# The statistics sums and the first two weight tiles of a projection, interleaved on TensorE

## The reference

```python
def rmsnorm(x, g):
    xf = x.astype(jnp.float32)
    y = xf * lax.rsqrt(jnp.mean(xf * xf, axis=-1, keepdims=True) + EPS)
    return (y * g.astype(jnp.float32)).astype(x.dtype)
...
x = x + 0.5 * rmsnorm(swiglu(rmsnorm(x, g[0]), w_ffn_gu[l, 0], w_ffn_down[l, 0]), g[1])
```

## Time and profile before

| | us |
|---|---|
| runs | 3531.46, 3548.50, 3548.51 |
| median | 3548.5 |
| span of the profiled execution | 3542.4 |
| TensorE busy in it | 3241.2 (91%) |
| VectorE, ScalarE busy | 1478.8 (42%), 1160.0 (33%) |
| mean granted TensorE clock | 0.950 of full |

### The profile page before, as it was taken

How to read it: one execution, slowest core, us unless ns; L and a number is a source line. 1 busy time by engine, 2 the same in 40 slices (tenths; PEclk the granted TensorE clock), 3 DMA queues, 4 the chain that set the end, 5 groups by cost and what they waited for, 6 DMA issues and landing times.

```text
span 3542.4 us, 55784 instructions
## 1 busy us (share of the span) xinstructions
PE 3241.2 (91%) x22328; PEld 2962.0 (84%) x22328; DVE 1478.8 (42%) x2113; ACT 1160.0 (33%) x1624; POOL 269.6 (8%) x364
## 2 busy tenths in 40 slices
PE   6999996998898898998999889999898878899997
PEld 5799996777677776798999879999896666899996
DVE  4444325655555512325443334443432051444423
ACT  3433323433333332324332214332222242333322
POOL 0000000211221110000000000000001101100000
PEclk9999997999989998999999999999999988999998
DMA  5422321222222223322232233332321611223321
GB/s 190 130 85 87 89 89 53 74 70 65 61 62 61 79 91 107 115 87 65 84 88 88 67 105 93 89 89 88 102 83 43 216 42 49 69 83 89 87 88 52
DMA packets 444917, 305.86 MB, mean 86 GB/s; under 512 B 12516, under 2 KB 415644, under 8 KB 444700
## 3 DMA queue, kind: packets, MB, share of 16 engines
q1 hardware_dynamic: 421780, 231.03, 22.3%
q0 software_dynamic: 19744, 69.48, 5.7%
q10 hardware_dynamic: 3328, 4.47, 0.4%
HBM read 282.73 MB, written 22.20 MB: 86 GB/s over the span
## 4 chain that ended last, share of the span: by engine, by line
PE 87%; DVE 7%; ACT 2%; issue 2%; DMA 1%; ACTq 0%; POOL 0%; SPq 0%; DVEq 0%; POOLq 0%
PE PS L894 64%; PE PS L945 5%; PE PS L932 2%; PE PS L1060 2%; PE PS L1072 1%; PE PS L1185 1%; PE PS L1033 1%; PE PS L1011 1%; DVE yT L1377 1%; DVE rb L1362 1%; PE PS L1187 1%; PE PS L1050 1%; PE PS L1250 1%; PE PS L1118 1%; PE PS L1197 1%
## 5 line engine op out<-in xcount | busy, mean ns | idle before, releaser
L894 PE MATMUL PS<-hH,whi 128*128 128x272 f32 x4048 | 842.8, 289 | 12.8 <-DVE hL L1373 7.6
L894 PE MATMUL PS<-hH,wlo 128*128 128x272 f32 x4048 | 837.8, 288 | 0.0
L894 PE MATMUL PS<-hL,whi 128*128 128x272 f32 x4048 | 837.0, 288 | 0.0
L1358 DVE TENSOR_TENSOR wlo<-raw,whi 128x1024 fp32r<-128x1024 f32 (+2 forms) x401 | 488.5, 1218 | 807.8 <-ACT whi L503 799.8
L503 ACT ACTIVATE whi<-raw 128x1024 fp32r<-128x1024 f32 (+2 forms) x401 | 413.1, 1030 | 766.3 <-PE PS L894 666.7
L894 PEld LDWEIGHTS PS<-hH,whi 128*128 128x128 f32 x4048 | 638.0, 189 | 14.9 <-issue 13.1
L894 PEld LDWEIGHTS PS<-hL,whi 128*128 128x128 f32 x4048 | 638.5, 189 | 0.0
L894 PEld LDWEIGHTS PS<-hH,wlo 128*128 128x128 f32 x4048 | 634.5, 189 | 0.0
L894 PE MATMUL PS<-H,whi 128*128 128x272 f32 x1984 | 411.9, 289 | 5.7 <-DVE L L1761 2.5
L894 PE MATMUL PS<-H,wlo 128*128 128x272 f32 x1984 | 411.0, 289 | 0.0
L894 PE MATMUL PS<-L,whi 128*128 128x272 f32 x1984 | 410.4, 288 | 0.0
(11 more groups left out here) (312 smaller groups left out, 3427.8 us busy)
## 6 DMA issues: line engine op xcount, KB each, us to landing
raw<-in_w_ffn_gu SPq DMA_DIRECT2D x176, 512.0 KB, 3.7
kvr<-in_cache_mem_kv POOLq DMA_DIRECT2D x32, 1024.0 KB, 5.5
raw<-in_w_in_a SPq DMA_DIRECT2D x57, 512.0 KB, 3.7
raw<-in_w_ffn_down SPq DMA_DIRECT2D x64, 448.0 KB, 3.3
rawm<-in_w_mem_kv SPq DMA_DIRECT2D x32, 512.0 KB, 4.2
raw<-in_w_ffn_down SPq DMA_DIRECT2D x32, 512.0 KB, 3.6
raw<-in_w_out_a SPq DMA_DIRECT2D x24, 512.0 KB, 3.5
raw<-in_w_in_b SPq DMA_DIRECT2D x20, 512.0 KB, 3.6
```

Source lines behind the costliest of these rows:

```text
L894: mm = pe.matmul(PS[:, bank + h, 0:HT], w[:, slot, k * P:(k + 1) * P], x(k0 + k)[:, h * HT:(h + 1) * HT], start=first and k == 0 and w is ...
L1358: dve.tensor_tensor(wlo[:, slot, 0:nk * P], src, whi[:, slot, 0:nk * P].bitcast(F32), ALU.subtract).then_inc(s["w_lo"], 1)
```

## The change

TensorE has a new function `first_pair`, which replaces the statistics and the first two units of each of the five projections: for each block it adds the square's sum and then that block's products for unit 0 and for unit 1. The last two blocks' sums come before their products. For this the split of unit 1 is moved ahead on both engines; the reciprocal is moved behind the split of unit 2; and the first pass of the gate/up loop is written out on ScalarE and VectorE. `residual` keeps the order of its additions, with one split ahead of it.

```diff
@@ ScalarE, end of narrow (the stage before)
+                if ahead is not None:
+                    split(ahead + 1, (ahead + 1) % 2)
@@ ScalarE, ffn
+                if f == 0:
+                    split(d.u0 + 1, (d.u0 + 1) % 2)
                 folded_h(gain(l, 4 * f))
...
+                        begun = first and b == 0
+                        if begun:
+                            split(u + 2, d.u0 % 2)
+                        else:
+                            split(u + 1, (d.u0 + 1) % 2)
                         act.wait_ge(evac[2 * b], i + e0[2 * b] + 2)
                         act.activation(sg[:, b, :], sg[:, b, :], ACT.Silu).then_inc(s["silu_done"], 1)
-                        split(u + 2, d.u0 % 2)
+                        if not begun:
+                            split(u + 2, d.u0 % 2)
...
-                step_loop(act, d.n, gu)
+                gu(0, True)
+                step_loop(act, d.n, gu, 1)
@@ TensorE
+            def first_pair(d):
...
+                for j in range(2):
+                    pe.wait_ge(evac[j], n.ev[j] + 1)
+                pe.wait_ge(s["w_lo"], d.u0 + 4)
+                def block(j, k):
+                    pe.wait_ge(*h_ready(k))
+                    mm = product((d.u0 + j) % 2, k, hH[:, k, :], hL[:, k, :], 2 * j, k == 0, k == KD - 1)
+                    if k == KD - 1:
+                        mm.then_inc(s["w_mm"], 1)
+                for k in range(KD):
+                    pe.wait_ge(s["sq_ready"], n.sq + k + 1)
+                    sums(sqf[:, k % 2, :], k == 0, k == KD - 1).then_inc(s["sq_used"], 1)
+                    if k < KD - 2:
+                        block(0, k)
+                        block(1, k)
+                for j in range(2):
+                    block(j, KD - 2)
+                    block(j, KD - 1)
...
@@ TensorE, dense
+                        if j < begun:
+                            seen[b] += 1
+                            continue
+                        if begun and j == 2:
+                            pe.wait_ge(s["rt_ready"], n.norm)
@@ VectorE, residual
+                if g_next:
+                    split(ahead + 1, (ahead + 1) % 2)
                 inverse()
@@ VectorE, ffn
+                d = ph["gu", l, f]
                 if f == 0:
+                    split(d.u0 + 1, (d.u0 + 1) % 2)
                     for k in range(KD):
                         folded_low(k, gain(l, 0))
                     n.t += KD
-                inverse(rtf)
...
+                        begun = first and b == 0
+                        if begun:
+                            split(u + 2, d.u0 % 2)
+                            inverse(rtf)
+                        else:
+                            split(u + 1, (d.u0 + 1) % 2)
                         dve.wait_ge(s["w_mm"], u + 3)
                         dve.tensor_tensor(halves(sg[:, b, :]), PS[:, 4 * b:4 * b + 2, 0:HT], halves(rb[:, :]), ALU.mult).then_inc(evac[2 * b], 1)
-                        split(u + 2, d.u0 % 2)
+                        if not begun:
+                            split(u + 2, d.u0 % 2)
@@ VectorE, in_b
+                    split(ph["in_b"].u0 + 2, ph["in_b"].u0 % 2)
                     inverse(rtf)
-                    queries(ph["in_b"], dst=M1, first=12, scale=HD ** -0.5)
+                    queries(ph["in_b"], 2, dst=M1, first=12, scale=HD ** -0.5)
```

More of the change, by code:

```diff
@@ L596, in to_h, with narrow @@
                 highs(y_of, hH_of, KD)
-            def narrow(d, early=0, last=False):
+            def narrow(d, early=0, last=False, ahead=None):
                 e = list(n.ev)
@@ L678, in ffn @@
                 dn = ph["down", l, f]
-                narrow(dn, last=(l, f) == (DEPTH - 1, 1))
+                narrow(dn, last=(l, f) == (DEPTH - 1, 1), ahead=ph["in_b"].u0 if (l, f) == (1, 0) else None)
             for l in range(DEPTH):
@@ L815, in _ @@
                     n.t += KI
-                    narrow(d, 2)
+                    narrow(d, 2, ahead=ph["gu", 0, 1].u0)
                 else:
                     folded_h(gain(1, 2))
-                    queries(ph["in_b"])
+                    queries(ph["in_b"], early=1)
                     queries(ph["qm", 1])
@@ L885, in _, with product @@
             n = Place()
+            def product(slot, k, hi_k, lo_k, bank, first, final):
+                for w, x in ((whi, hi_k), (whi, lo_k), (wlo, hi_k)):
+                    for h in range(2):
+                        mm = pe.matmul(PS[:, bank + h, 0:HT], w[:, slot, k * P:(k + 1) * P],
+                                       x[:, h * HT:(h + 1) * HT],
+                                       start=first and w is whi and x is hi_k, stop=final and w is wlo)
+                return mm
             def products(slot, nk, k0, hi, lo, bank, first, final, ready=None):
@@ L891, in products, with dense, body @@
                         pe.wait_ge(*ready(k0 + k))
[L892 to L897, removed]
-                return mm
-            def dense(d, hi, lo, pos=lambda j: j, ready=None, summed=False):
+                    mm = product(slot, k, hi(k0 + k), lo(k0 + k), bank, first and k == 0, final and k == nk - 1)
+                return mm
+            def first_pair(d):
+                n.t += KD
+                n.unscaled += KD
+                for j in range(2):
[15 more added lines that the diff above has]
+                    block(j, KD - 1)
+                n.sq += KD
+                n.norm += 1
+            def dense(d, hi, lo, pos=lambda j: j, ready=None, summed=False, folded=False):
+                if folded:
+                    first_pair(d)
                 e = list(n.ev)
-                def body(i):
+                def body(i, begun=0):
                     seen = [0] * 4
@@ L916, in body @@
                                      None if j else ready).then_inc(s["w_mm"], 1)
-                step_loop(pe, d.n, body)
+                if folded and d.tiles > 2:
+                    body(0, 2)
+                step_loop(pe, d.n, body, int(folded))
                 if summed:
+                    n.norm += 1
                     pe.wait_ge(evac[2], n.ev[2] + 1)
@@ L1080, in ffn @@
             def ffn(l, f):
-                folded_stats()
-                dense(ph["gu", l, f], hH_of, hL_of, ready=h_ready)
+                dense(ph["gu", l, f], hH_of, hL_of, folded=True)
                 dense(ph["down", l, f], lambda k: H24[:, k, :], lambda k: L24[:, k, :], ready=lambda k: (s["mid_lo"], n.mid + k + 3), summed=True)
@@ L1231, in _ @@
                 else:
-                    folded_stats()
-                    dense(ph["in_b"], hH_of, hL_of, ready=h_ready)
+                    dense(ph["in_b"], hH_of, hL_of, folded=True)
                     dense(ph["qm", 1], hH_of, hL_of)
```

38 lines of the change are left out of this document (17 added, 21 removed).

## The result

The kernel after takes 3565.4 us (median of 5 runs, 3563.6 to 3570.4), the kernel before 3548.5 (5 runs, 3531.5 to 3548.7). The ratio is 1.0063, 95% interval 1.0047 to 1.0079. The forecast was 3571.5, range 3553 to 3585, "slower by over 0.5%" at 0.63. The low end of the interval lies just under that half per cent, the middle above it. The ratio is taken over all the runs; the two medians are 16.9 us or 0.48% apart. Two of before's five runs lie 13 to 17 us under the others, and in 21 and 22 later runs its median was 3546.3 and 3545.9, 19 to 20 us under the changed kernel's. So the direction and the size are as forecast; that the ratio comes out at 0.63%, and not nearer to half a per cent, is owed in part to before's two low runs.

What follows compares the result with a forecast made beforehand. TensorE was taken as the bound, busy for 91% of the span. Work moved forward (-13.0), waits behind the pair (18.9 + 5.6) and clock falls (+11.5) gave +23.0 on 3548.5 us: 3571.5, range 3553 to 3585.

Steps and rivals of the forecast that it cites:

- slower by over 0.5%: Whole kernel: a time above 3566.2 us, chance 0.63.
- end of the pair: When units 0 and 1 are done at five projection starts: changes -0.2, -3.3, -0.1, -4.3 and -5.1 us, together -13.0.
- moved forward, with the clock of (0,0): Five projection starts: pairs end 13.0 us earlier together, against 1.2 us for the clock's fall at (0,0).
- unit 3 after the pair's end, four times: Four gate/up projections: unit 3 starts 10.8 us after the pair's end instead of 6.06, with TensorE idling 3.65.
- unit 2 of in_b after the pair's end: In in_b, unit 2 waits for unit 0's bank, read after the reciprocal, and starts 5.6 us after the pair.
- lost behind the pair: Waits after the pair's end: 18.9 us over four gate/up projections plus 5.6 us in in_b.
- clock, without (0,0): Clock falls after waits behind the pair: 8.0 us before unit 3 in four projections, 2.3 in in_b.
- The pass: At five starts, sums and first pair take 19.5 us at full clock, plus half of the half-clock time.
- The path behind unit 0: From unit 0's end: split of unit 2, reciprocal, gate tile, split of unit 3; unit 3 starts 12.3 us after.
- The clock: TensorE falls to half clock after the new idle times: 8.0 + 2.3 + 1.2 = +11.5 us, bounds 0 and 18.
- The clock holds: Rival: the idle times come, but the clock does not fall after them; +11.5 us, 3560; chance 0.22.
- The lock step: Rival: in the pass, squares wait for sums behind two blocks' products; 2.4 us a projection, +12, 3583; chance 0.10.

Runs made afterwards that it cites:

- e2: Changed kernel with a plain copy in place of the reciprocal of the five folded norms: 3541.7 us, ratio to before 0.9992.
- e5: Changed kernel with the split of unit 3 moved ahead of unit 0's gate tile on both engines: 3546.8 us, ratio to before 0.9998.
- e6: Changed kernel with only two blocks of unit 1 woven in, its other six after unit 0: 3543.9 us, ratio to before 0.9995.
- e3: Changed kernel with unused extra matmuls in TensorE's waits, 10 before unit 2 in in_b, 6 before unit 3 elsewhere: 3558.3 us, ratio to before 1.0042.
- e7: Changed kernel with e4, e5 and e6 together: 3531.8 us, ratio to before 0.9958.
- e8: e7 with unit 1's split after the second block at (0,0) and (1,0), TensorE waiting for it only before unit 1: 3531.9 us, ratio to before 0.9956.
- e9: e8 with sums first and tiles after, not woven, in gate/up of (0,0) and (1,0): 3531.3 us, ratio to before 0.9962.
- e4: Changed kernel with the reciprocal ahead of the split of unit 2 in VectorE's queue, gate/up and in_b: 3558.4 us, ratio to before 1.0045.

## Why the prediction was right, step by step

Times of the kernel after are moved back by the distance of the stage's first restart from that of before (0.55, 9.03, 12.02, 18.12 and 19.21 us), so that they stand beside the prediction's.

| term | predicted | measured |
|---|---|---|
| end of the pair, (0,0) | 163.4, and 1.2 of clock | 165.2 |
| (0,1) | 1624.2 | 1624.0 |
| (1,0) | 2160.6 | 2160.7 |
| in_b | 2577.6 | 2578.0 |
| (1,1) | 3106.0 | 3105.9 |
| moved forward, with the clock of (0,0) | -11.8 | -11.1 |
| unit 3 after the pair's end, four times | 10.8 | 10.5 |
| unit 2 of in_b after the pair's end | 5.6 | 5.3 |
| lost behind the pair | +24.5 | +23.0 |
| clock, without (0,0) | +10.3 | +9.3 |
| sum | +23.0 | +21.2 |

The forward ends are 1624.2 - 1627.5 and so on; the measured ones, against the same readings of before, are +1.6, -3.5, 0.0, -4.0 and -5.2. The sum of the terms, 21.2, meets the five stages' 21.5.

- **The pass.** The sum of sums and blocks at 0.92 and 0.757, with half of the half-clock time on top, gave four ends within 0.4 us. Its miss is (0,0): the start came at 144.06 in place of 143.9, and the clock fell there for 3.4 us (1.7) where I had taken 1.2 between nothing and more. The half-clock times in it, 5.8, 4.9 and 3.7, are the 6.1 and 4.0 of the earlier trace rows less the delay of each start, which the prediction doesn't say; that the spell ends where it ended before was an assumption. The kernel after shows 5.8, 5.1 and 4.9, and 4.9 at (1,1), where only one spell is left, as forecast. So at in_b 1.2 us more were at half clock than assumed, and that is the whole miss there.
- **The path behind unit 0.** Its order and members were as predicted. It is 0.3 us shorter; I had added handovers of 0.1 and 0.2 at each step. The wait before unit 3 came out at 3.14 us instead of 3.65. e2, e5 and e6 cut it, break it up and start it earlier, and each takes back 16 to 24 us.
- **The clock.** I took 2.0 for each wait before unit 3, because 3.65 was longer than the five in the trace; at 3.14 it wasn't longer than the 3.36 there, and it cost 1.7 each time, as after 2.6 us at the earlier trace rows. "The clock holds" (0.22) didn't happen: e3 shows what it would have brought, 8.1. The Trainium skill (TensorE: Matmul & The Clock Gate, "HAM oscillation — how this bites in real kernels") has each wait between bursts pay anew. The trace agrees at the five waits of 3.1 us and more behind the pairs; after the four of 1.1 us, and after the 3.36 us at 2085.64, nothing was paid.
- **The lock step** (0.10) didn't come: the pass at (0,1) took 22.35 us where 22.4 were forecast, with no wait of over 0.35 us in it.
- **The two numbers of one execution.** 3571.5 is 6.1 above the measured median. I took the profiled execution's own time as 6.1 above its span. In every run listed since, it is 1.7 above, so before's was 3544.1, 4.4 under the median that I added to, and with my 23.0 the forecast from it is 3567.1. I had compared the span of one execution with the median of others. Taken apart in another way: against the forecast of 23.0 the five stages grew by 21.5, the two spans by 19.5 and the two medians by 16.9. So 1.5 of the 6.1 lie in the changed stages; the rest lies outside them (2.0) and in the spread of the runs (2.6).

The spread of the kernel before was underrated rather than wrong: in later runs beside the experiments it lay between 3530.8 and 3553.9. e7, e8 and e9 lie at 3528.0 to 3534.2 in all their 16 runs. That is 14.4 under before's median, of which the five stages account for 10.4 in e7's trace, and no better than before's lowest runs. The other 4 are not shown to come from the edits.

## What to carry to other kernels

When work is interleaved so that two units finish together, look at what is released by the *first* of them. Whatever was hidden behind the second is now bare; here a path of 12 us hung on the end of unit 0, and letting unit 1 finish only two blocks behind it uncovered the path. Finish one unit early and let the other fill the gaps: that alone brought the kernel back to the time before (e6), and with the path shortened as well the whole gain was kept (e7). A queue that works in order turns "after the split, which has to wait anyway" into a serial chain, so a long instruction (3.55 us among ones of 0.7 to 1.2) belongs ahead of the first wait that its operand allows. And weaving is worth only what idles: 3 to 5 us behind a residual, under 1 where the pass is paced by ScalarE's squares.

## What the runs showed that I had not expected

**Table loads.** The change wrote out the first pass of ScalarE's gate/up loop. Groups of the kernel before, then of after:

```profile
L503 ACT ACT_TABLE_LOAD x44 | 56.5, 1283 | 0.8
L669 ACT ACT_TABLE_LOAD x44 | 56.5, 1283 | 0.8
```

```profile
L678 ACT ACT_TABLE_LOAD x4 | 5.1, 1283 | 0.1
```

88 loads of 1.28 us became 4, one a stage. ScalarE's busy time fell by 109 us for it, and the kernel gained nothing from it that can be seen: from unit 3 of (0,1) to the end of stage B the kernel after takes 382.4 us, 1.7 of them by the clock's fall, and the kernel before 380.9. ScalarE isn't what ends the waits of those loops. The Trainium skill (ScalarE activation tables: per-element evaluation and per-set limits, "Table sets in the compiler and the runtime") says that the compiler's back end places loads block by block; that a peeled first pass removes them from a loop's body fits that, but no run here isolates it.

**The clock's edge.** After 1.32 us of idle TensorE the first sum of (0,0) ran at full clock before the change; after 1.41 us, with the same stretch of work ahead of it, it was at 1.2 GHz for 3.4 us in e8 and e9. After 1.42 at unit 3 (e6) it held. Before unit 2 of in_b it fell after 2.15 us in e2 (a mean of 0.79 in the 8 us from 2585.7) and held after 2.26 in e6. In the kernel before, seven waits of 1.65 to 1.86 us in the first 125 us held, and after eight of 1.8 us in the scan the 8 us that follow have a mean of 0.79. The length of a wait alone doesn't decide it, and what does is open.

**The layer-1 attention.** From its first transposes to the statistics after out(1) the profiled executions take 381 to 386 us, but 372 in e2 and e4, with no edit there. That is about the distance of the low runs from the high ones of the kernel before. The stretch in the kernel before and in e2:

```profile
2691.40:3075.50 384.10, 324.70 (x1756) 258.25 (x1756) 103.71 (x180) 108.43 (x183) 55.61 (x88) 0.89 0.28 90
```

```profile
2696.70:3068.70 372.00, 312.64 (x1756) 251.55 (x1756) 103.72 (x180) 108.49 (x184) 55.60 (x88) 0.93 0.29 92
```

The matmuls are the same, and TensorE is idle for the same 59.4 us in both; the same matmuls took 12.1 us less, at a mean clock of 0.93 instead of 0.89 (0.92 in e4, 0.88 to 0.90 in the eight other kernels). So the two levels of this stretch are the granted clock and no wait. It also fits the list of whole runs: before's later runs under 3533 us have a mean clock of 0.953 to 0.955, those over 3545 one of 0.946 to 0.951. Why the clock falls less in some executions is open.
